# Two transformer blocks on one core: the second block's pools, borders and attention woven into the steps of its networks

## The reference

```python
h_lat, h_ctx = x, ctx
for i in range(2):
    sh1, sc1, g1, sh2, sc2, g2 = split(silu(c) @ ada_w[i] + ada_b[i], 6)       # for lat
    csh1, csc1, cg1, csh2, csc2, cg2 = split(silu(c_ctx) @ ada_w[i] + ada_b[i], 6)  # for ctx
    a_l = modulate(rms_norm(h_lat, norm_g[i, 0]), sh1, sc1)
    a_c = modulate(rms_norm(h_ctx, norm_g[i, 0]), csh1, csc1)
    if i == 0:                      # windows of 2, 4, 8, 16 tokens, one for each 256 columns
        y_l, y_c = pool_mix(a_l, pool_w, pool_scale), pool_mix(a_c, pool_w, pool_scale)
    else:                           # q, k normed by head; rope on lat alone; k, v of both
        y_c, y_l = attn_mix(a_c, a_l, w_qkv, w_o, q_g, k_g, ctx_out=False)
    h_lat = h_lat + g1 * y_l
    m_l = modulate(rms_norm(h_lat, norm_g[i, 1]), sh2, sc2)
    h_lat = h_lat + g2 * (square(relu(m_l @ w1[i])) @ w2[i])
    if i == 0:
        h_ctx = h_ctx + cg1 * y_c
        m_c = modulate(rms_norm(h_ctx, norm_g[i, 1]), csh2, csc2)
        h_ctx = h_ctx + cg2 * (square(relu(m_c @ w1[i])) @ w2[i])
return rms_norm(h_lat, final_g)
```

## Time and profile before

| | us |
|---|---|
| median of 3 runs | 2154.43 (2154.2 to 2154.57) |
| profiled execution, its own time | 2153.26 |
| its span in the profile | 2151.5 |
| TensorE busy | 1962.9 (91%) |
| VectorE busy | 1170.0 (54%) |
| ScalarE busy | 945.8 (44%) |

### The profile page before, as it was taken

The page is one execution under the profiler, slowest core; times in us unless marked ns, Lnnn a source line. Parts: engine busy times, 40 slices in busy tenths (PEclk is TensorE's granted clock), DMA queues, the critical chain, the costliest instruction groups (busy, mean ns, idle before and its releaser), DMA issues.

```text
span 2151.5 us, 23289 instructions
## 1 busy us (share of the span) xinstructions
PE 1962.9 (91%) x9499; PEld 1574.9 (73%) x9503; DVE 1170.0 (54%) x1351; ACT 945.8 (44%) x1293; POOL 96.5 (4%) x157
## 2 busy tenths in 40 slices
PE   4999975899999999999999995799999989698997
PEld 3777864677777777887877774588778877576885
DVE  3544665454456444855554456654565555745553
ACT  3444533344445444644544444444454445324442
POOL 2300000100001000000000001000000000000000
PEclk9999986799999999999999997899999999899999
DMA  7777640376657776554576652155535545213551
GB/s 223 241 235 247 209 141 1 105 258 229 229 179 238 235 235 225 181 174 160 190 264 228 228 200 79 42 195 195 176 137 195 183 135 171 88 49 128 183 187 60
DMA packets 233881, 379.63 MB, mean 176 GB/s; under 512 B 11960, under 2 KB 152512, under 8 KB 233776
## 3 DMA queue, kind: packets, MB, share of 16 engines
q1 hardware_dynamic: 231376, 369.82, 51.0%
q0 software_dynamic: 2400, 8.33, 1.5%
HBM read 377.06 MB, written 1.05 MB: 176 GB/s over the span
## 4 chain that ended last, share of the span: by engine, by line
PE 85%; DVE 8%; ACT 4%; issue 1%; DMA 1%; POOL 1%; SPq 0%; DVEq 0%; POOLq 0%; ACTq 0%
PE ps L451 25%; PE ps L453 24%; PE ps L452 24%; PE ps L461 5%; PE ps L597 2%; DVE w_lo L1594 1%; DMA tmp<-pool_scale_dram 1%; PE ps L1106 1%; PE ps L976 1%; PE ps L1085 1%; ACT arena L1159 1%; DVE tmp L2048 1%; ACT w_hi L1138 0%; DVE xt_lo L1613 0%; PE ps L1031 0%
## 5 line engine op out<-in xcount | busy, mean ns | idle before, releaser
L1594 DVE TENSOR_TENSOR w_lo<-raw,w_hi 128x1024 fp32r<-128x1024 f32 x602 | 719.4, 1226 | 266.4 <-ACT w_hi L1138 265.6
L1138 ACT ACTIVATE w_hi<-raw 128x1024 fp32r<-128x1024 f32 x602 | 614.5, 1055 | 294.4 <-PE ps L453 278.8
L451 PE MATMUL ps<-w_hi,xt_hi 128*128 128x512 f32 x1632 | 648.3, 397 | 15.4 <-DVE xt_lo L1603 7.6
L453 PE MATMUL ps<-w_hi,xt_lo 128*128 128x512 f32 x1632 | 637.1, 390 | 0.0
L452 PE MATMUL ps<-w_lo,xt_hi 128*128 128x512 f32 x1632 | 636.5, 390 | 0.0
L451 PEld LDWEIGHTS ps<-w_hi,xt_hi 128*128 128x128 f32 x1632 | 308.6, 189 | 81.7 <-DVE w_lo L1594 7.8
L453 PEld LDWEIGHTS ps<-w_hi,xt_lo 128*128 128x128 f32 x1632 | 308.3, 189 | 65.0
L452 PEld LDWEIGHTS ps<-w_lo,xt_hi 128*128 128x128 f32 x1632 | 308.8, 189 | 62.6 <-issue 1.9
L451 PE MATMUL ps<-w_hi,ht_hi 128*128 128x512 f32 x768 | 306.4, 399 | 7.1 <-DVE ht_lo L2072 7.1
L452 PE MATMUL ps<-w_lo,ht_hi 128*128 128x512 f32 x768 | 300.1, 391 | 0.0
L453 PE MATMUL ps<-w_hi,ht_lo 128*128 128x512 f32 x768 | 299.7, 390 | 0.0
(11 more groups left out here) (264 smaller groups left out, 1113.2 us busy)
## 6 DMA issues: line engine op xcount, KB each, us to landing
raw<-mlp_w_dram SPq DMA_DIRECT2D x192, 512.0 KB, 4.3
raw<-ffn_w_in_dram SPq DMA_DIRECT2D x176, 512.0 KB, 5.6
arena<-ada_w_dram SPq DMA_DIRECT2D x96, 512.0 KB, 6.4
raw<-ffn_w_out_dram SPq DMA_DIRECT2D x88, 512.0 KB, 4.5
raw<-odd_w_in_dram SPq DMA_DIRECT2D x48, 512.0 KB, 4.7
raw<-attn_w_qkv_dram SPq DMA_DIRECT2D x24, 512.0 KB, 4.7
raw<-even_w_in_dram SPq DMA_DIRECT2D x22, 512.0 KB, 4.7
raw<-ple_w_gate_dram SPq DMA_DIRECT2D x16, 512.0 KB, 4.4
```

Source lines behind the costliest of these rows:

```text
L451: pe.matmul(dst, a_hi, hi, start=start, stop=False)
L453: return pe.matmul(dst, a_lo, hi, start=False, stop=stop)
L1138: act.activation(w_hi[:, slot, c], raw[:, slot, c], ACT.Copy).then_inc(S(f"hi{slot}"), 1)
L1594: TT(w_lo[:, slot, c], raw[:, slot, c], w_hi[:, slot, c].bitcast(F32), ALU.subtract).then_inc(S(f"lo{slot}"), 1)
```

## The change

- **Start.** SP issues the identity alone and tile 0 of `x`, then the first four halves of weights, then the rest. The six vectors go to ScalarE's queue; GpSimd's four loads wait until the first step of ffn(0) has been computed up (`f_up0` at 2). The first splits of weights stand between those of `x` on both engines.
- **ple(l).** The rows of `proj` for tile 0 move behind the gate rows of tile 1.
- **Pools.** The ctx pool (turns, window sums, rows by `pool_w`, its gate row) becomes jobs in the steps of ffn(3), `ctx_job`. The ctx network runs first, from ple(1) on, and the lat pool becomes jobs in its steps, `lat_job`. Then the lat network, with gate rows and the turns of ctx for attention in its steps. The two `mlp(0)` swap places and nothing else of their size changes. Window sums are formed for one group of 256 columns at a time.
- **Borders.** `up_tiles` computes the first products of a network tile by tile: tile 1 is turned (`xn_fill`, 16 by `x2_turn` and `x2_split`) while tile 0 is multiplied. `gated_add` and the norms go by tile too.
- **Gate rows.** TensorE multiplies a column of the modulation, spread over 128 columns, by the identity; the diagonal matrices, the ones and `clear` are gone.
- **Attention.** Chunk order ctx 2, 3, then lat 2, 0, 1, 3. Squares of heads on ScalarE (`head_squares`) for each chunk; gains are folded into the rope tables and the softmax's scale. The turns, scores and weighted sums stand among the chunks and among the rows of `w_o`.
- **End.** The last network finishes tile 0 first; its update, norm and store go by tile.

The core of the diff:

```diff
+            sp.dma_start(const[:, 0:C_TRI], T["const_tab"][:, 0:C_TRI]).then_inc(S("ident_in"), 16)
+            sp.dma_start(h_lat[:, 0], T["x"][0, 0:P]).then_inc(S("x_in0"), 16)
+            def first_tables():
+                sp.dma_start(h_lat[:, 1], T["x"][0, P:2 * P]).then_inc(S("x_in1"), 16)
...
+                if run == 0:
+                    first_tables()
...
-            for c in (0, 1, 2, 3, 2, 3):
+            for c in (2, 3, 2, 0, 1, 3):
...
+            def gate_row(l, part, v, halves, b0):
+                pe.wait_ge(S("mod_set"), l + 1)
+                for half in halves:
+                    for k in range(4):
+                        g = ada_of(l, part, v)[:, 4 * half + k:4 * half + k + 1].to_broadcast([P, P])
+                        last = pe.matmul(ps[:, b0 + half, k * P:(k + 1) * P], g, ident, start=True, stop=True)
+                    last.then_inc(S("gate_ps"), 1)
...
+            def ctx_job(i):
+                if i == 0:
+                    gate_row(0, 2, 1, (1,), 5)
+                elif i < 5:
+                    if i == 1:
+                        wait_xn()
+                    pool_turn(xn_c, i - 1, 6)
+                elif i < 9:
+                    pool_rows(xn_c, 0, (i - 5) // 2, (i - 5) % 2, 6)
...
+            def up_tiles(out0, sig0, f=None, at=(), do=None):
+                slots = (ring.take(), ring.take())
+                for m in range(MT):
+                    for k in range(KT):
+                        slot, uses = slots[k // 4]
+                        if m == 0 and k % 2 == 0:
+                            slab(slot, uses, k // 2 % 2)
+                        if (m, k) == at:
+                            do()
+                        if f is not None:
+                            pe.wait_ge(S("x2_lo"), 2 * (f + m) + k // 4 + 1)
+                        last = three(bank(out0 + m), xt_hi[:, k, m * P:(m + 1) * P], xt_lo[:, k, m * P:(m + 1) * P],
...
-                proj_rows(0, 6)
                 acc_is_free()
                 for k in range(4):
                     gate_rows(1, k)
+                proj_rows(0, 6)
                 proj_rows(1, 4)
                 gate += [ring.take(), ring.take()]
                 for m in range(MT):
                     for k in range(4, KT):
+                        if l and (m, k) == (1, 6):
+                            wait_xn()
+                            pe.wait_ge(S("z_ready"), 2 * l + 1)
+                            xn_fill(0, xn_c)
...
+            def mlp(job, job_read, last=False):
                 base = MLP_STEPS * n["mlp"]
                 n["mlp"] += 1
-                wait_xn()
-                xt_fill(xn, of_h=True)
-                gain_row()
-                up(4, "m_up0", wait_xt=True)
-                pe.wait_ge(S("gain_set"), n["gain"])
-                clear(0)
-                def down(i, final):
-                    pe.wait_ge(S("m_ht"), base + i + 1)
-                    add_rows(ht_hi, ht_lo, 0, False, False)
-                    add_rows(ht_hi, ht_lo, 2, False, final)
-                def step(i):
+                for i in range(MLP_STEPS - 1):
                     hidden("m_", base + i, 4)
                     up(4, "m_up0")
-                    down(i, False)
-                ring.loop(pe, MLP_STEPS - 1, 4, step)
+                    pe.wait_ge(S("m_ht"), base + i + 1)
+                    if i == 0:
+                        acc_is_free()
+                    job(i)
+                    add_rows(ht_hi, ht_lo, 0, i == 0, False)
+                    add_rows(ht_hi, ht_lo, 2, False, False)
+                    job_read(i)
...
+            def lat_job(i):
+                if i == 0:
+                    gate_row(0, 2, 0, (0, 1), 6)
+                elif i < 3:
+                    if i == 1:
+                        wait_xn()
+                    for b in range(2):
+                        pool_turn(xn_l, 2 * (i - 1) + b, 6 + b)
+                elif i < 5:
+                    for half in range(2):
+                        pool_rows(xn_l, 1, i - 3, half, 6 + half)
+                elif i == 5:
+                    gate_row(0, 5, 1, (0, 1), 6)
+                elif i == 7:
+                    wait_xn()
+                    xn_fill(0, xn_l)
+                elif i == 8:
+                    xn_fill(1, xn_l)
...
+            up_tiles(6, "pj0", at=(1, 6), do=lat_fill)
+            chunk_free(2)
+            up_tiles(4, "pj0", f, (0, 2), lambda: xn_fill(1, xn_l, b0=2))
+            pe.wait_ge(S("a_kc"), 1)
+            turn_heads(YCK, 0)
+            chunk_free(3)
+            up(6, "pj0")
+            pe.wait_ge(S("a_rope"), 1)
+            turn_heads(YK, 2)
+            chunk_free(4)
+            up(4, "pj0")
+            pe.wait_ge(S("a_rope"), 2)
+            pe.wait_ge(S("a_T"), 2)
+            turn_heads(YQ[0], 0)
+            chunk_free(5)
+            def first_scores():
+                pe.wait_ge(S("a_T"), 6)
+                scores(0)
+            up_tiles(6, "pj0", at=(1, 0), do=first_scores)
+            n["pj"] += 6
+            pe.wait_ge(S("pj_act"), n["pj"] - 1)
+            pe.wait_ge(S("pj_dve"), n["pj"] - 1)
+            pe.wait_ge(S("a_rope"), 3)
+            turn_heads(YQ[1], 4)
+            turn_weights(0)
+            pe.wait_ge(S("a_T"), 8)
+            pe.wait_ge(S("pj_act"), n["pj"])
+            pe.wait_ge(S("pj_dve"), n["pj"])
+            scores(1)
+            weigh(0)
+            scores(2)
+            turn_weights(1)
+            weigh(1)
+            turn_weights(2)
+            scores(3)
+            weigh(2)
+            out_fill(0, 2)
...
+            out_rows(0, 0)
+            turn_weights(3)
+            out_rows(0, 1)
+            weigh(3)
+            out_rows(0, 2, (0,))
+            out_fill(1, 6)
+            out_rows(0, 2, (1,))
+            out_rows(1, 0)
+            out_rows(1, 1)
+            out_slots.append(ring.take())
+            out_rows(0, 3).then_inc(S("acc0"), 1)
             n["epi"] += 1
-            mlp(xn_lat)
+            out_rows(1, 2)
+            out_rows(1, 3)
...
+            def norm(h, upd, count, xn):
+                act.wait_ge(S(upd), count)
+                squares(lambda m: h[:, m, :])
+                xn_tile0(h, xn)
...
+            def head_squares(y, c, cols):
+                act.wait_ge(S("pj_act"), n["pj"] + c + 1)
+                act.wait_ge(S("pj_dve"), n["pj"] + c + 1)
+                for m in range(MT):
+                    for h in range(4):
+                        i = cols + 4 * m + h
+                        last = act.activation(junk[:, (4 * m + h) * P:(4 * m + h) * P + P], y[:, m, h * P:(h + 1) * P], ACT.Square,
+                                              accum_out=ssq_h[:, i:i + 1])
+                last.then_inc(S("a_sq"), 1)
...
+            def pool_sums(xn, g):
+                dve.wait_ge(S("p_t"), n["pool"] + 1)
+                n["pool"] += 1
+                w = SEQ + 2 * PAD
+                step(TT(B[:, :, 1:w], A[:, :, 0:w - 1], A[:, :, 1:w], ALU.add))
+                if g > 0:
+                    step(TT(C[:, :, 2:w - 1], B[:, :, 1:w - 2], B[:, :, 3:w], ALU.add))
+                if g > 1:
+                    step(TT(B[:, :, 4:w - 3], C[:, :, 2:w - 5], C[:, :, 6:w - 1], ALU.add))
+                if g > 2:
+                    step(TT(C[:, :, 8:w - 8], B[:, :, 4:w - 12], B[:, :, 12:w - 4], ALU.add))
+                sums = (B, C, B, C)[g][:, :, PAD:PAD + SEQ]
+                dve.wait_ge(S("inv_in"), 32)
+                step(TT(sums, sums, over(inv_cnt[g // 2][:, g % 2], 1, 2), ALU.mult))
+                to = xn[:, :, 2 * g * P:(2 * g + 2) * P].rearrange("p m (k j) -> p k m j", k=2)
+                TT(to, sums.rearrange("p k (m j) -> p k m j", m=2),
+                   A[:, :, PAD:PAD + SEQ].rearrange("p k (m j) -> p k m j", m=2), ALU.subtract).then_inc(S("pooled"), 1)
...
+            def gated_add(m, h, gate, gates, upd, k_back):
+                dve.wait_ge(S("gate_set"), gates)
+                if m == 0:
+                    dve.wait_ge(S("acc0"), n["epi"] + 1)
+                else:
+                    slot, uses = ring.back(k_back)
+                    dve.wait_ge(S(f"used{slot}"), 2 * uses)
+                gated_products(m, gate)
+                gated_sums(m, h, upd)
...
+            gated_add(0, h_lat, table, 10, "h_upd", 2)
+            split((0,))
+            dve.wait_ge(S("rstd"), 2 * n["sq"] - 1)
+            dve.tensor_scalar(xn_l[:, 0, :], h_lat[:, 0, :], rstd[:, k, 0:1], None, ALU.mult).then_inc(S("xm"), 1)
+            split((1,))
+            gated_add(1, h_lat, table, 10, "h_upd", 3)
...
+            act.dma_start(a[0:112, 0, :], T["norm_g"].rearrange("l n (k c) -> (l n k) c", c=P)).then_inc(S("vec_in"), 16)
...
+            act.dma_start(a[48:56, 2, :], T["pool_scale_2"].rearrange("b (k c) -> (b k) c", c=P)).then_inc(S("vec_in"), 16)
...
+            pool.wait_ge(S("f_up0"), 2)
             load_gain(0, 1)
```

1016 lines of the change are left out of this document (621 added, 395 removed).

## The result

The changed kernel takes 2056.75 us (median of 4 runs, 2055.59 to 2056.86), the kernel before 2154.5 beside it; the ratio is 0.9544 (95% interval 0.9532 to 0.9556), 97.8 us less. Forecast were 2052.4 in a range from 2037 to 2073.

The account below looks back on a forecast made before the run. The prediction took TensorE to bound the kernel, with only its idle or slow time to win. Its terms summed to −102.0 us, from 2154.4 to 2052.4, in a range from 2037 to 2073.

Parts of the forecast that it names:

- What bounds it: Whole kernel: the last-ending chain lies on TensorE for 85% of the span; only its idle or slow time can be won.
- Start: Kernel start: weights first and GpSimd's loads deferred bring the first product from 28.78 to 12.3 to 12.8 us; −16.
- The bound of 4: Kernel start: if the DMA hole stayed, only the loads that move behind would be saved, some 4 us.
- ple: Both ple stages: gate rows ahead of proj cover the low-part waits and slow matmuls; −5.8 us, 0 if cover fails.
- Jobs: Pool and gate work moved into network steps: ffn(3) +10.3, ctx network +14.8, lat network +5.7, last +1.9 us.
- Pool stretch: From ple(1) to the ctx network's first turned step: 85.4 us becomes 20.9, with a wait of 5.6; −64.5.
- Borders and attention: Border between networks 21.6 to 15.3 us, −6.3; attention with its two borders to 164.9, −40.8.
- Rival 2: Attention: head chain longer than its cover, 3 us late at four chunks and the softmax; +15, 2067 us; chance 0.13.
- Last network: Last network: gate-row work moved into its steps adds 1.9 us.
- Not placed: Anywhere: some thirty new small hand-overs at 0.1 us each; +3, bounds 0 and 8.
- Rival 5: Loaded steps: mixed work holds TensorE at 1.2 GHz, slower than before; seven such steps +134, 2187 us; chance 0.03.

Follow-up runs that it names:

- e10: Changed kernel with GpSimd's four loads issued at the very start, ahead of its first 1/rms; 2066.66 us, +9.9.
- e11: Changed kernel with GpSimd's loads at the very start and the tables ahead of the first weights on SP; 2070.59 us, +13.8.
- e5: Changed kernel with the proj rows of tile 0 ahead of the gate rows of tile 1 again in both ple; 2062.08 us, +5.3.
- e8: Changed kernel with each matmul of the pool rows issued twice; 2069.99 us, +13.2.
- e7: Changed kernel with the additions of the window sums done twice on VectorE; 2064.32 us, +7.6.
- e3: Changed kernel with a network's first relu and its square ahead of the other token set's norm, in ctx and lat networks; 2048.02 us, −8.7.
- e9: Changed kernel with eight more multiplications of 0.42 us on VectorE in the rope of each of three lat chunks; 2066.06 us, +9.3.

## Why the prediction was right, point by point

**What bounds it.** Right: TensorE's share rose from 91% to 95%. Its idle time fell from 188.6 to 112.5 us, 76.1 of the 98.2 in the spans; the other 22.1 are busy time, slow matmuls and dropped work (the diagonal products, `clear`).

**Start.** −16 stood, and e10 shows the main reason, GpSimd's loads. First product at 14.48, not 12.3 to 12.8: the last half of weights landed at 11.7, near the 11.4 worked out, but both its splits and then a low part of x (the 2.68 us wait for L1937) stood ahead of it. This was offset behind it, where the wait of 0.62 went and the some 16 slow matmuls became some ten. So −16.2 is right by two sizes that cancel, the smaller part by luck. The bound of 4 for a hole that stays was low: with the loads at once a gain of 6 us is left (e10), with the tables ahead as well 2 (e11).

**ple.** −1.8 and −4.2 for −1.7 and −4.1. e5 brings 1.9 back at each: it shows the cause in ple(0), and in ple(1) for less than half. The larger wait and the slow matmuls behind it did not return with the old order, so for those 2.3 us no run shows the cause.

**Jobs.** 11.2 for 10.3 in ffn(3). The term mis-sized is the gate row there: I took one half row at 0.95, but two halves stand in that stage; by the n-th matmul one costs 0.9, the other 2.2, since the turns behind it wait for ScalarE (0.75 and 1.51 us; before, one wait of 0.97 stood there). The turns in fours took 0.41 for 0.55, pool rows 1.65 for 1.79. In the ctx network 15.8 for 14.8, of which 1.4 is slow clock behind its last wait. e8 shows that a job's price is TensorE's time, e7 that the cover on VectorE was 0.5 us at the tightest place, as said.

**Pool stretch.** −64.0 for −64.5; the wait was 6.0 for 5.6 worked out. e3 shows the cause of 3.4 of it, the norm; the 2.6 that stay come from relu and its square, which nothing precedes in e3 but a slab's splits.

**Borders and attention.** −5.7 for −6.3 and −39.6 for −40.8. The sum was right by two errors that offset each other. TensorE was busy 148.4 of 166.0 us where I had worked out 154.2 of work, and the waits, 17.8 us, were larger than the 11.4 that I placed: 3.7 ahead of lat's first chunk, where I had 1 (its turned tile stood behind the head squares), 2.1, 0.9 and 1.2 around scores and `w_o`, and 1.3 + 6.3 + 1.0 + 1.4 at the last border for 8. The head chain made no wait: the turn of k stands 0.1 us behind its rope, and e9 shows that each microsecond more would have counted. Rival 2 was near.

The work was mis-sized in the turns: 144 instructions in this window (16 of the 160 had moved into the lat network) took 16.6 us for 26.7, 0.115 each. My price, 2.67 for 16, was no work of TensorE. Those turns stand behind the exponentials, and in the kernel before each four of them wait for the next:

```profile
1871.83 0.42 PEld L461 LDWEIGHTS ps<-const,arena 128*128 128x128 f32 x4 [0.35 <-ACT arena L1553]
1872.50 0.42 PEld L461 LDWEIGHTS ps<-const,arena 128*128 128x128 f32 x4 [0.25 <-ACT arena L1553]
```

Four turns take 0.44 us there and start every 0.67. A row gives a price only where the engine wasn't paced by another one; the earlier trace rows had it, 0.79 for eight. Against this the 432 matmuls took 103.4 us for 98.4, by slow ones behind the waits and switches.

**Last network.** 3.4 for 1.9: a spell of eight slow matmuls behind the last wait, 1.7.

**Not placed.** I had put 3 for small hand-overs. They were not what came; the even mixer's 1.9 and the spells of slow clock (3.1 in two networks) were. That the term fits is luck.

**Rival 5, the clock.** It did not come: a loaded stretch of the ctx network, from 1355 to 1405, with turns, pool rows and window sums:

```profile
1355.00:1405.00 50.00, 50.00 (x236) 41.87 (x235) 38.26 (x43) 25.67 (x33) 0.00 (x0) 1.00 0.48 173
```

Clock 1.00, 2.4 GHz, with TensorE busy throughout. The rule of the Trainium skill on transposes (TensorE: Matmul & The Clock Gate, Part 4: PE-mode transpose) did not show here either.

## What to carry to other kernels

Work of small stages went into the steps of a long stage at the price of TensorE's own time, so the gain is the waits of the stage taken apart; count the margin of the fullest step on each other engine, since here it was half a microsecond. At a border, ask for each waiting engine what stands ahead of the awaited operation in its list and whether that is needed sooner: two such moves gave 6.9 and 3.1 us at their places in a kernel already rewritten. Gains to be added are read at their places, not from the times of whole runs. Loads that a start doesn't need are worth holding back, first of all those of small pieces on GpSimd's queue (9.9 to 10.8 us here; the tables on SP's queue 3.0 to 3.9), and an operation that is moved ahead of them holds them back as well as a wait does.
